# Dilated attention on TensorE: the two heads of a pair take turns block by block, on opposite halves of the array

## The chip, the cores and the metric

The kernel runs on one core of one Trainium2 chip. The metric is the device time of one execution in microseconds (us), as the median of several runs. TensorE is PE in the rows (its weight loads are PEld), VectorE is DVE, ScalarE is ACT, GpSimd is POOL, and SyncE, which issues the weight transfers, is SP.

## The reference, cut to what matters

The model is two blocks of several layers over 512 tokens of width 1024. The change touches one stage of the second block: attention with a causal dilated window. There are twelve heads of width 64 in three groups of four, with (window, dilation) of (128, 1), (512, 4) and (2048, 16).

```python
qb = to_sub(q).reshape(bb, nb, ATTN_BLOCK, h, dh)          # ATTN_BLOCK = 128
kb = band(to_sub(k)); vb = band(to_sub(v))                  # own block and the one before
scores = jnp.einsum('bnqhd,bnkhd->bnhqk', qb, kb) * (dh ** -0.5)
scores = jnp.where(mask[None, :, None], scores, -jnp.inf)
m = jnp.max(scores, axis=-1, keepdims=True)
p = jnp.exp(scores - m)
denom = jnp.sum(p, axis=-1, keepdims=True)
o = jnp.einsum('bnhqk,bnkhd->bnqhd', (p / denom).astype(v.dtype), vb)
lse = (m + jnp.log(denom))[..., 0]
```

The output of a head is its read-out `o` and the logarithm `lse` of its denominator; later the three groups are weighed by a softmax over their `lse`.

## The kernel before

Everything is transposed: channels lie on the 128 partitions, tokens along the free axis. Two heads of width 64 share a tile of 128 partitions, head r = 0 on partitions 0 to 63 and head r = 1 on 64 to 127. Such a tile is called a pair (index u, two of them in each group), and a group (index g) has a stage of its own. The tokens are handled as four blocks of 128 (NB = 4). In group 0 a block of queries sees two blocks of keys (WB = 256), in groups 1 and 2, where the tokens are sorted by residue, only one (WB = 128).

A stage (`dilated_attention`) runs two programs on each engine, woven by a list of turns: the attention of the group (`Dilated`) and a projection that the next stages need (`Flow`). The flow is the bulk of TensorE's work: for each of six output tiles, eight turns of three products of 512 columns (L459, fp32r; the weights are split in an upper part on ACT, L337, and a lower part on DVE, L378). The list spreads the twenty turns of `Dilated` over those of the flow. Within an engine the order is fixed; between engines semaphores decide. A block barrier ends each stage.

For each pair, the attention does this:

- ACT copies the queries, keys and values to tiles of their own (L3202), TensorE turns the values over (L3288), ACT takes them (L3207).
- TensorE makes the scores of head 0 into `ps_s[0]`, and one turn of the list later those of head 1 into `ps_s[1]` (L3298). The queries of a block are the stationary operand, 64 rows by 128 columns, so a head uses only one half of the array's rows. `scored` counts the heads.
- DVE scales and masks a head's scores (L3242), takes the maximum (L3245) and subtracts it (L3247); ACT takes the exponential (L3212). DVE sums (L3254), inverts (L3256) and norms (L3258), head 0 before head 1.
- TensorE turns the probabilities over (L3308), once `normed` says that DVE is done with them; in the first pair of a stage it first runs 12, 9 or 4 products that nobody reads (L57, `keep_busy`). ACT takes them as `pt` (L3220) and spreads the logarithms of the denominators to `lrow` (L3222).
- TensorE makes the read-outs of head r (L3320 for the block before, L3323 for the own block) and its denominators (L3329). Here the stationary operand is 128 rows by 64 columns, and head r writes partitions 64r to 64r + 63 of `ps_o` and of `ps_l` (the latter is `ps_v` in the rows). Head 0 has one turn of the list, head 1 the next.
- DVE and ACT take read-outs and denominators (L3271, L3228), which ends the pair (`turn_done`).

Each 128-column product of type f32 stands in the trace as two loads and two matmuls; a transpose stands there once.

Of the kernel before, what the change touches and what calls it, by code (L numbers as in the profile page):

```python
# [10 lines left out]
P = 128  # L11
# [203 lines left out]
class Flow:  # L215
# [152 lines left out]
    def dve(self, dve):  # L368
# [39 lines left out]
        yield from self.turns(dve, first, events)  # L408

    def pe(self, pe):  # L410
        K, nc = self.K, self.K.nc

# [61 lines left out]
def product(K, name, w, n, kt, rhs_hi, rhs_lo, t0, T, on_act, on_dve, nxt, extra="", side=None, rms_of=None,  # L474
            busy=0):

    nc = K.nc
    with ExitStack() as c:
        f = Flow(K, c, name, w, n, kt, rhs_hi, rhs_lo, t0, T, on_act, on_dve, nxt, extra, side, rms_of)
        unread = c.enter_context(nc.psum_tensor(f"{name}_unread", [P, 512], F32))[:, 0:P] if busy else None  # L480
        with K.block() as block:
            @block.sync
            def _(sp):
                weave([], f.sp(sp))

            @block.gpsimd
            def _(pool):
                if side is not None:
                    side[0].pool(pool)

            @block.scalar
            def _(act):
                weave([], f.act(act))

            @block.vector
            def _(dve):
                weave([], f.dve(dve))

            @block.tensor
            def _(pe):  # L500
                weave([], f.pe(pe))
                if busy:
                    K.keep_busy(unread, busy)
# [2632 lines left out]
class Dilated:  # L3136
# [139 lines left out]
    def pe(self, pe):  # L3276
        nc, K, g, NB, WB = self.nc, self.K, self.g, self.NB, self.WB
        ident = K.ident[:, :]

        def block_of(t, b):  # L3280
            return t[:, b * P:(b + 1) * P]
        for u in range(2):
            if u > 0:
                pe.wait_ge(self.turn_done, u)
            yield
            pe.wait_ge(self.v_in, u + 1)
            for b in range(NB):
                last = nc.tensor.transpose(block_of(self.ps_v, b), block_of(self.vs, b), ident)  # L3288
            last.then_inc(self.v_turned, 1)
            yield  # L3290
            pe.wait_ge(self.qk_in, u + 1)
            for r in range(2):
                half = slice(64 * r, 64 * r + 64)
                for b in range(NB):
                    first = b if g else max(b - 1, 0)
                    spans = [(b * WB, b * P)] if g else [(b * WB, first * P), (b * WB + P, b * P)]
                    for col, key in spans:
                        last = nc.tensor.matmul(self.ps_s[r][:, col:col + P], self.qs[half, b * P:(b + 1) * P],  # L3298
                                                self.ks[half, key:key + P], start=True, stop=True)
                last.then_inc(self.scored, 1)  # L3300
                yield
            yield
            for r in range(2):
                if u == 0 and r == 0:
                    K.keep_busy(self.ps_o[:, 0:P], (12, 9, 4)[g])
                pe.wait_ge(self.normed, 2 * u + r + 1)
                for b in range(self.WS // P):
                    last = nc.tensor.transpose(block_of(self.ps_s[r], b), self.p[:, r, b * P:(b + 1) * P], ident)  # L3308
                last.then_inc(self.p_turned, 1)
                yield  # L3310
            pe.wait_ge(self.vt_in, u + 1)
            for r in range(2):
                n = 2 * u + r
                half = slice(64 * r, 64 * r + 64)
                pe.wait_ge(self.pt_in, n + 1)
                for b in range(NB):
                    both = g == 0 and b > 0
                    if both:
                        at = (b - 1) * P + 64 * r
                        nc.tensor.matmul(self.ps_o[half, b * P:(b + 1) * P], self.vt[:, at:at + 64],  # L3320
                                         self.pt[:, r, b * WB:b * WB + P], start=True, stop=False)
                    at = b * P + 64 * r
                    last = nc.tensor.matmul(self.ps_o[half, b * P:(b + 1) * P], self.vt[:, at:at + 64],  # L3323
                                            self.pt[:, r, (b + 1) * WB - P:(b + 1) * WB], start=not both, stop=True)
                if r:
                    last.then_inc(self.o_done, 1)
                pe.wait_ge(self.rows, n + 1)
                for b in range(NB):
                    last = nc.tensor.matmul(self.ps_l[half, b * P:(b + 1) * P], self.lrow[:, r, b, :], ident,  # L3329
                                            start=True, stop=True)  # L3330
                if r:
                    last.then_inc(self.l_done, 1)
                yield
            yield


# [506 lines left out]
```

## Time and profile before

| | |
|---|---|
| Median of 3 runs | 2849.68 us (2845.45 to 2850.74) |
| The profiled execution | 2852.88 us |
| Its span in the trace | 2851.1 us |
| PE busy | 2660.7 us, 93% of the span |
| DVE, ACT busy | 1666.8 us (58%), 1007.7 us (35%) |
| Granted TensorE clock, mean | 0.979 of full speed |
| The three dilated stages | 2480 to 2659 us of the span |

Read the table so: TensorE is the engine that is nearly always busy, and the three stages of the change are 179 us, 6% of the span. Whether a change of TensorE's work there moves the end is seen from where TensorE itself waits inside those stages.

### The profile page before, as it was taken

What the parts mean: (1) busy time and instruction counts of PE and PEld (TensorE: products, weight loads), DVE (VectorE), ACT (ScalarE), POOL (GpSimd) and SP (SyncE); (2) the same over time, 40 slices, a digit from 0 to 9 for tenths busy, and PEclk for the clock granted to TensorE, in tenths of its full rate; (3) what the DMA queues carried; (4) which work ended last, traced back from release to release, by engine and by line L of the source; (5) the groups of instructions that cost most, each with busy time, mean ns of one, the idle gap of its engine ahead of it and who ended that gap; (6) DMA issues with size and microseconds to landing.
All of it is one profiled execution on the core that took longest, in us unless ns stands there. A gap on an engine that the chain in (4) does not pass through costs nothing. (4 is left out here: it accounts for less than half of the span.)

```text
span 2851.1 us, 37621 instructions
## 1 busy us (share of the span) xinstructions
PE 2660.7 (93%) x15331; PEld 2237.1 (78%) x15331; DVE 1666.8 (58%) x2729; ACT 1007.7 (35%) x1392; POOL 55.4 (2%) x108
## 2 busy tenths in 40 slices
PE   7999888999999999889999999988889897999997
PEld 3888787888888888756579999866778886877786
DVE  4888774466667766443347657466655563343634
ACT  4226545332212223344343323255422223334532
POOL 0100000000010000000000000000000000000000
PEclk9999999999999999999999999999999998999999
DMA  6640002223343332210034443212200000211232
GB/s 230 194 152 16 23 9 80 91 83 95 116 150 104 101 108 81 86 38 8 1 104 138 156 127 114 96 59 74 77 8 16 16 9 30 96 56 58 73 99 78
DMA packets 61950, 231.62 MB, mean 81 GB/s; under 512 B 6865, under 2 KB 9553, under 8 KB 61138
## 3 DMA queue, kind: packets, MB, share of 16 engines
q1 hardware_dynamic: 46802, 174.68, 18.5%
q0 software_dynamic: 14976, 54.53, 6.0%
q8 instruction: 122, 2.00, 0.3%
q14 instruction: 50, 0.41, 0.0%
HBM read 227.08 MB, written 2.10 MB: 80 GB/s over the span
## 5 line engine op out<-in xcount | busy, mean ns | idle before, releaser
L378 DVE TENSOR_TENSOR w_lo<-w_raw,w_hi 128x1024 fp32r<-128x1024 f32 (+4 forms) x284 | 346.9, 1221 | 395.6 <-ACT w_hi L337 392.6
L337 ACT ACTIVATE w_hi<-w_raw 128x1024 fp32r<-128x1024 f32 (+4 forms) x284 | 297.7, 1048 | 224.2 <-PE late_acc L459 87.2
L459 PE MATMUL mid_acc<-mid_h_hi,w_hi 128*128 128x258 f32 x832 | 279.4, 336 | 1.5 <-DVE mid_od_fq L627 1.0
L459 PE MATMUL mid_acc<-mid_h_hi,w_lo 128*128 128x258 f32 x832 | 279.0, 335 | 0.0
L459 PE MATMUL mid_acc<-mid_h_lo,w_hi 128*128 128x258 f32 x832 | 277.1, 333 | 0.0
L459 PE MATMUL late_acc<-late_h_hi,w_hi 128*128 128x258 f32 x704 | 199.3, 283 | 0.0
L459 PE MATMUL late_acc<-late_h_hi,w_lo 128*128 128x258 f32 x704 | 198.4, 282 | 0.0
L459 PE MATMUL late_acc<-late_h_lo,w_hi 128*128 128x258 f32 x704 | 197.6, 281 | 0.0
L459 PEld LDWEIGHTS mid_acc<-mid_h_hi,w_hi 128*128 128x128 f32 x832 | 157.3, 189 | 19.3 <-issue 2.4
L459 PEld LDWEIGHTS mid_acc<-mid_h_lo,w_hi 128*128 128x128 f32 x832 | 157.5, 189 | 18.6 <-issue 1.2
L459 PEld LDWEIGHTS mid_acc<-mid_h_hi,w_lo 128*128 128x128 f32 x832 | 156.8, 188 | 16.1
L459 PEld LDWEIGHTS late_acc<-late_h_lo,w_hi 128*128 128x128 f32 x704 | 133.6, 190 | 0.5 <-issue 0.5
L459 PEld LDWEIGHTS late_acc<-late_h_hi,w_hi 128*128 128x128 f32 x704 | 133.1, 189 | 0.5 <-issue 0.5
L459 PEld LDWEIGHTS late_acc<-late_h_hi,w_lo 128*128 128x128 f32 x704 | 132.7, 188 | 0.0
L459 PE MATMUL mid_acc<-mid_y_hi,w_hi 128*128 128x256 f32 (+1 forms) x384 | 128.8, 335 | 3.5 <-DVE w_lo L378 1.9
L459 PE MATMUL mid_acc<-mid_y_lo,w_hi 128*128 128x256 f32 (+1 forms) x384 | 128.9, 336 | 0.0
L459 PE MATMUL mid_acc<-mid_y_hi,w_lo 128*128 128x256 f32 (+1 forms) x384 | 128.7, 335 | 0.0
L131 DVE CUSTOM_DVE_ANT_0 mid_scratch<-mid_side_raw,mid_rows 128x1024 f32<-128x1024 f32 x96 | 117.4, 1223 | 1.7
L459 PE MATMUL dq_acc<-s_h_hi,w_hi 128*128 128x512 f32 x200 | 87.7, 438 | 20.8 <-DVE w_lo L378 16.6
L2906 ACT ACTIVATE dr_low<-dr_bank 128x512 f32<-128x512 f32 x48 | 28.7, 598 | 169.7 <-PE dr_bank L3036 169.7
L459 PE MATMUL qvz_acc<-ev_h_hi,w_hi 128*128 128x256 f32 (+1 forms) x256 | 87.2, 341 | 1.5 <-DVE ev_h_lo L921 1.5
L459 PE MATMUL qvz_acc<-ev_h_lo,w_hi 128*128 128x256 f32 (+1 forms) x256 | 86.9, 339 | 0.0
(563 smaller groups left out, 6309.4 us busy)
## 6 DMA issues: line engine op xcount, KB each, us to landing
w_raw<-in_up SPq DMA_DIRECT2D x88, 512.0 KB, 3.5
mid_side_raw<-in_ada_t POOLq DMA_DIRECT2D x48, 512.0 KB, 3.8
w_raw<-in_down SPq DMA_DIRECT2D x32, 704.0 KB, 4.0
qvz_side_raw<-in_ada_t POOLq DMA_DIRECT2D x32, 512.0 KB, 3.8
w_raw<-in_dn_qkv SPq DMA_DIRECT2D x25, 512.0 KB, 3.2
late_side_raw<-in_ada_t POOLq DMA_DIRECT2D x24, 512.0 KB, 3.8
w_raw<-in_da SPq DMA_DIRECT2D x18, 512.0 KB, 3.3
w_raw<-in_ev_qvz SPq DMA_DIRECT2D x16, 512.0 KB, 3.5
```

Of the source, the lines that this page charges most:

```text
L131: nc.vector.tensor_tensor_reduce(out=self.scratch, in0=self.raw[:, j, :], in1=self.rows[:, m, :], scale=1.0, scalar=0.0, op0=ALU.mult, op1 ...
L337: nc.scalar.activation(K.whi[:, g % 2, 0:width], K.raw[:, g % 2, 0:width], ACT.Copy).then_inc(K.hi_done, 1)
L378: nc.vector.tensor_tensor(K.wlo[:, g % 2, 0:width], K.raw[:, g % 2, 0:width], K.whi[:, g % 2, 0:width].bitcast(F32), ALU.subtract).then_in ...
L459: last = nc.tensor.matmul(self.acc[i % len(self.acc)][:, at:at + width], left[:, j, cols], right[k][:, moving:moving + width], start=(k == ...
L2906: nc.scalar.activation(XL[G][:, :], bank[G][0][:, :], ACT.Copy).then_inc(A[G].empty, 1)
```

## The change

The loops over blocks and heads change places. The scores of both heads of a pair are now one burst, in which the heads alternate for each block of keys; the burst stands in the turn of head 0, and `scored` is raised by 2 at its end. The read-outs and the denominators of both heads are likewise one burst, in the turn of head 1. No product is added or taken away, and nothing changes on the other engines.

```diff
-            for r in range(2):
-                half = slice(64 * r, 64 * r + 64)
-                for b in range(NB):
-                    first = b if g else max(b - 1, 0)
-                    spans = [(b * WB, b * P)] if g else [(b * WB, first * P), (b * WB + P, b * P)]
-                    for col, key in spans:
+
+            for b in range(NB):
+                first = b if g else max(b - 1, 0)
+                spans = [(b * WB, b * P)] if g else [(b * WB, first * P), (b * WB + P, b * P)]
+                for col, key in spans:
+                    for r in range(2):
+                        half = slice(64 * r, 64 * r + 64)
                         last = nc.tensor.matmul(self.ps_s[r][:, col:col + P], self.qs[half, b * P:(b + 1) * P],
                                                 self.ks[half, key:key + P], start=True, stop=True)
-                last.then_inc(self.scored, 1)
-                yield
+            last.then_inc(self.scored, 2)
+            yield
+            yield
             yield
...
-            for r in range(2):
-                n = 2 * u + r
-                half = slice(64 * r, 64 * r + 64)
-                pe.wait_ge(self.pt_in, n + 1)
-                for b in range(NB):
-                    both = g == 0 and b > 0
-                    if both:
+            pe.wait_ge(self.pt_in, 2 * u + 1)
+            yield
+
+            pe.wait_ge(self.pt_in, 2 * u + 2)
+            for b in range(NB):
+                both = g == 0 and b > 0
+                if both:
+                    for r in range(2):
                         at = (b - 1) * P + 64 * r
...
-                pe.wait_ge(self.rows, n + 1)
-                for b in range(NB):
-                    last = nc.tensor.matmul(self.ps_l[half, b * P:(b + 1) * P], self.lrow[:, r, b, :], ident,
-                                            start=True, stop=True)
-                if r:
-                    last.then_inc(self.l_done, 1)
-                yield
+            last.then_inc(self.o_done, 1)
+            pe.wait_ge(self.rows, 2 * u + 2)
+            for b in range(NB):
+                for r in range(2):
+                    last = nc.tensor.matmul(self.ps_l[64 * r:64 * r + 64, b * P:(b + 1) * P], self.lrow[:, r, b, :],
+                                            ident, start=True, stop=True)
+            last.then_inc(self.l_done, 1)
+            yield
```

The first pair of group 0 on TensorE, before: the scores of the two heads (`da_ps_s`, eight products a head) with three turns of the flow between them.

```order
L459 MATMUL da_acc<-s_h_hi,w_lo 128x512
L3298 MATMUL da_ps_s<-da_ks,da_qs 128x128 x8
L459 MATMUL da_acc<-s_h_hi,w_hi 128x512
L459 MATMUL da_acc<-s_h_lo,w_hi 128x512
L459 MATMUL da_acc<-s_h_hi,w_lo 128x512
...
L3298 MATMUL da_ps_s<-da_ks,da_qs 128x128 x8
```

And in the changed kernel, where the same line is L3299:

```order
L459 MATMUL da_acc<-s_h_hi,w_hi 128x512
L459 MATMUL da_acc<-s_h_lo,w_hi 128x512
L459 MATMUL da_acc<-s_h_hi,w_lo 128x512
L3299 MATMUL da_ps_s<-da_ks,da_qs 128x128 x16
L459 MATMUL da_acc<-s_h_hi,w_hi 128x512
```

The sixteen products stand where the first eight stood; the second place is gone, so head 0's scores are complete eight products later in TensorE's order, and head 1's nine products of the flow earlier.

The read-outs and denominators of the same pair on TensorE, before: this group of rows stands there twice, once for each head, with three turns of the flow between.

```order
L3323 MATMUL da_ps_o<-da_pt,da_vt 64x128
L3320 MATMUL da_ps_o<-da_pt,da_vt 64x128
L3323 MATMUL da_ps_o<-da_pt,da_vt 64x128
L3320 MATMUL da_ps_o<-da_pt,da_vt 64x128
...
L3329 MATMUL da_ps_v<-ident,da_lrow 64x128 x4
```

In the changed kernel (L3323 is now the block before, L3327 the own block, L3333 the denominators):

```order
L3327 MATMUL da_ps_o<-da_pt,da_vt 64x128 x2
L3323 MATMUL da_ps_o<-da_pt,da_vt 64x128 x2
L3327 MATMUL da_ps_o<-da_pt,da_vt 64x128 x2
L3323 MATMUL da_ps_o<-da_pt,da_vt 64x128 x2
...
L3333 MATMUL da_ps_v<-ident,da_lrow 64x128 x8
```

Each x2 is head 0 and head 1 in turn. The whole burst stands at the place of head 1's, with nine more products of the flow ahead of it than head 0's had.

## Rows read from the trace of the kernel before

**Rows 1.** The page: span and busy time of each engine.

```profile
span 2851.1 us, 37621 instructions
...
PE 2660.7 (93%) x15331; PEld 2237.1 (78%) x15331; DVE 1666.8 (58%) x2729; ACT 1007.7 (35%) x1392; POOL 55.4 (2%) x108
```

**Rows 2.** Sum over the three stages: length, busy time of each engine.

```profile
sum 179.00, PE 165.01 PEld 133.28 DVE 80.69 ACT 74.16 POOL 0.00; mean PE 55.00 PEld 44.43 DVE 26.90 ACT 24.72 POOL 0.00
```

**Rows 3.** Groups by shape, 2480 to 2659: count, busy us, mean ns, idle before.

```profile
L3298 PE MATMUL da_ps_s<-da_ks,da_qs 64*128 64x128 f32 x128 | 17.4, 281 | 0.0
L3298 PEld LDWEIGHTS da_ps_s<-da_ks,da_qs 64*128 64x128 f32 x128 | 15.1, 187 | 4.3 <-issue 4.3
L3323 PE MATMUL da_ps_o<-da_pt,da_vt 128*64 128x128 f32 x96 | 15.0, 279 | 0.0
L3329 PE MATMUL da_ps_v<-ident,da_lrow 128*64 128x128 f32 x96 | 12.4, 273 | 0.0
...
L3323 PEld LDWEIGHTS da_ps_o<-da_pt,da_vt 128*64 128x64 f32 x96 | 10.5, 136 | 4.3 <-issue 4.3
...
L3320 PE MATMUL da_ps_o<-da_pt,da_vt 128*64 128x128 f32 x24 | 4.6, 272 | 0.0
```

**Rows 4.** Timeline of PE, group 0, first pair: start, us from first to last.

```profile
2485.34 0.40 PE L459 MATMUL da_acc<-s_h_hi,w_lo 128*128 128x512 f32 x1
2485.66 2.05 PE L3298 MATMUL da_ps_s<-da_ks,da_qs 64*128 64x128 f32 x16
2487.64 0.50 PE L459 MATMUL da_acc<-s_h_hi,w_hi 128*128 128x512 f32 x1
2487.98 0.39 PE L459 MATMUL da_acc<-s_h_lo,w_hi 128*128 128x512 f32 x1
2488.21 0.40 PE L459 MATMUL da_acc<-s_h_hi,w_lo 128*128 128x512 f32 x1
...
2499.54 1.10 PE L3308 MATMUL da_ps_s<-ident,da_p 128*128 128x128 f32 x8 [1.27 <-DVE da_p L3258]
```

**Rows 5.** Timeline of PEld, the read-outs of the same pair.

```profile
2504.91 0.19 PEld L3323 LDWEIGHTS da_ps_o<-da_pt,da_vt 128*64 128x64 f32 x2 [0.36 <-issue]
...
2506.39 0.90 PEld L3329 LDWEIGHTS da_ps_v<-ident,da_lrow 128*64 128x64 f32 x8
```

**Rows 6.** Timeline of DVE, the same pair: each head's scores, and when they come.

```profile
2487.83 1.23 DVE L3242 SCALAR_TENSOR_TENSOR da_p<-da_ps_s,da_msk 128x1024 f32<-128x1024 f32 x1 [4.62 <-PE da_ps_s L3298]
...
2492.01 1.23 DVE L3242 SCALAR_TENSOR_TENSOR da_p<-da_ps_s,da_msk 128x1024 f32<-128x1024 f32 x1 [0.45 <-PE da_ps_s L3298]
```

**Rows 7.** Timelines of DVE and PE, group 0, second pair.

```profile
2526.66 1.22 DVE L3242 SCALAR_TENSOR_TENSOR da_p<-da_ps_s,da_msk 128x1024 f32<-128x1024 f32 x1
...
2533.05 1.97 PE L3308 MATMUL da_ps_s<-ident,da_p 128*128 128x128 f32 x8 [3.35 <-DVE da_p L3258]
```

**Rows 8.** PE in two stretches there: length, busy us, granted clock, DMA.

```profile
2529.70:2533.05 3.35, 0.01 (x1) 0.94 0.00 0
2533.05:2536.00 2.95, 2.95 (x11) 0.50 0.00 0
```

**Rows 9.** Timelines of DVE and PE, group 1, first pair.

```profile
2559.06 0.69 DVE L3242 SCALAR_TENSOR_TENSOR da_p<-da_ps_s,da_msk 128x512 f32<-128x512 f32 x1 [1.14 <-PE da_ps_s L3298]
...
2563.17 0.69 DVE L3258 TENSOR_TENSOR da_p<-da_p,da_inv 128x512 f32<-128x512 f32 x1
...
2564.49 0.60 PE L3308 MATMUL da_ps_s<-ident,da_p 128*128 128x128 f32 x4
```

**Rows 10.** Timelines of DVE and PE: group 1, second pair, and group 2, first pair.

```profile
2591.65 0.69 DVE L3258 TENSOR_TENSOR da_p<-da_p,da_inv 128x512 f32<-128x512 f32 x1
...
2592.40 0.66 PE L3308 MATMUL da_ps_s<-ident,da_p 128*128 128x128 f32 x4
...
2619.53 0.66 PE L3308 MATMUL da_ps_s<-ident,da_p 128*128 128x128 f32 x4 [0.38 <-DVE da_p L3258]
```

More of the change, by code:

```diff
@@ L3311, in pe @@
             pe.wait_ge(self.vt_in, u + 1)
-            for r in range(2):
-                n = 2 * u + r
-                half = slice(64 * r, 64 * r + 64)
-                pe.wait_ge(self.pt_in, n + 1)
-                for b in range(NB):
-                    both = g == 0 and b > 0
-                    if both:
+            pe.wait_ge(self.pt_in, 2 * u + 1)
[5 more added lines that the diff above has]
+                    for r in range(2):
                         at = (b - 1) * P + 64 * r
-                        nc.tensor.matmul(self.ps_o[half, b * P:(b + 1) * P], self.vt[:, at:at + 64],
+                        nc.tensor.matmul(self.ps_o[64 * r:64 * r + 64, b * P:(b + 1) * P], self.vt[:, at:at + 64],
                                          self.pt[:, r, b * WB:b * WB + P], start=True, stop=False)
+                for r in range(2):
                     at = b * P + 64 * r
-                    last = nc.tensor.matmul(self.ps_o[half, b * P:(b + 1) * P], self.vt[:, at:at + 64],
+                    last = nc.tensor.matmul(self.ps_o[64 * r:64 * r + 64, b * P:(b + 1) * P], self.vt[:, at:at + 64],
                                             self.pt[:, r, (b + 1) * WB - P:(b + 1) * WB], start=not both, stop=True)
-                if r:
-                    last.then_inc(self.o_done, 1)
-                pe.wait_ge(self.rows, n + 1)
-                for b in range(NB):
-                    last = nc.tensor.matmul(self.ps_l[half, b * P:(b + 1) * P], self.lrow[:, r, b, :], ident,
-                                            start=True, stop=True)
-                if r:
-                    last.then_inc(self.l_done, 1)
-                yield
+            last.then_inc(self.o_done, 1)
+            pe.wait_ge(self.rows, 2 * u + 2)
+            for b in range(NB):
+                for r in range(2):
+                    last = nc.tensor.matmul(self.ps_l[64 * r:64 * r + 64, b * P:(b + 1) * P], self.lrow[:, r, b, :],
+                                            ident, start=True, stop=True)
+            last.then_inc(self.l_done, 1)
+            yield
             yield
```

## The prediction

> **What bounds the kernel now.** I read the page first: TensorE is busy for 93% of the span, DVE for 58%, ACT for 35% [rows 1], so the end moves with TensorE's own order of work. In the sum over the three dilated stages it is busy for 165.0 of 179.0 us [rows 2]. The groups by shape then give what the change handles: 128 records of scores, and 96 + 24 + 96 = 216 records of read-outs and denominators; a product of 128 columns is two records [rows 3]. Last come the timelines. The reader is to see two things there: how fast such records follow each other, and where TensorE waits for DVE. It does so at the first transposes of a pair (L3308): 1.27 us in the first pair of group 0 [rows 4], 3.35 in its second [rows 7], 0.38 in the first pair of group 2 [rows 10]. Those waits say where time won on TensorE is worth nothing, and where scores that come late cost their full delay.
>
> **The pace of the records.** The burst of sixteen score records lasts 2.05 us [rows 4]. Its last matmul begins about 0.27 before its end and its first stream about 0.10 after its start, so a record takes (2.05 - 0.37) / 15 = 0.112. The loads of the denominators, eight in 0.90 us with a mean of 0.137 [rows 3, 5], follow each other every (0.90 - 0.137) / 7 = 0.109 us. Where no stream is in the way, at the start of the read-outs, the second of two loads of 64 columns begins 0.19 - 0.137 = about 0.054 after the first [rows 5]. So a load of 64 columns holds the loading path for 0.054, the stream of 128 columns is what makes 0.109. A load of 128 columns (187 ns against 136 [rows 3]) is 0.051 longer, about 0.105: in the scores load and stream are about equally long and lie under each other.
>
> **The change, part by part.** Between bursts and the flow there is a toll. Into the scores, the step from the last product of the flow is 2485.66 - 2485.34 = 0.32 instead of 0.23; out of them, the last record begins at 2485.66 + 0.10 + 15 x 0.112 = 2487.44, the flow at 2487.64 and its second product 0.34 later, so 0.09 + 0.11 too much [rows 4]. Together 0.30. The change removes one of two bursts of scores and one of two of read-outs in each of six pairs.
>
> No row shows alternating halves, so their pace is bounded from both sides: 0.109 to 0.112 (nothing overlaps; what rows 4 and 5 show) down to half of it (two halves stream at once), and above it what a load costs that no stream covers, 0.054 or 0.105 more. I take for the forecast that the halves stream together but that there is one loading path, since that is the only limit besides the stream that the rows show. Then a read-out or denominator record costs its load, 0.055, and a score record still about 0.110.
>
> *Read-outs and denominators.* 216 x (0.109 - 0.055) = 11.7 us, and six tolls of 0.30 = 1.8. Nothing hides TensorE's time there: after them it goes on with the flow, and the next waits (for the values' copies, a chain on ACT that starts from a flow tile of TensorE and moves with it) shift along. The probabilities and the logarithms' rows that the burst needs are made by ACT while the nine more products of the flow run. Gain 13.5.
>
> *Scores.* Here something is late. DVE's first head begins when the burst of its scores ends, and now that burst is both heads': 16 records more in group 0 (16 x 0.112 = 1.8 us), 8 in groups 1 and 2 (0.9). Queued behind this wait on DVE are the scaling, maximum and subtraction of both heads, the flow's L378, and the sum, inverse and norm of head 0, for which TensorE's L3308 waits.
> - Group 0, first pair: head 0's three steps end at 2492.01 - 0.45 = 2491.56 and DVE then waited 0.45 for head 1 [rows 6]. Now 1.8 later and without that wait: +1.4 us at L3308, all of it on TensorE, which waits there already.
> - Group 0, second pair: DVE goes through without a wait [rows 7], so the whole 1.8.
> - Group 1, first pair: DVE waited 1.14 for head 1 [rows 9], more than 0.9. DVE is done at 2563.86, TensorE comes at 2564.49 [rows 9]: not bound by DVE, it keeps its toll, -0.3. Group 2, first pair, waits 0.38 for the same chain [rows 10]: 1.14 - 0.9 = 0.2 earlier, -0.2.
> - Second pairs of groups 1 and 2 (one pattern): norm done at 2592.34, L3308 at 2592.40 [rows 10], DVE-bound: +0.9 each.
>
> Sum: 1.4 + 1.8 - 0.3 - 0.2 + 0.9 + 0.9 = +4.5 us. The toll saved there is lost in the waits.
>
> *The clock.* In the 2.95 us after the wait of 3.35, during which TensorE had done nothing, the granted clock is 0.50, that is 1.2 instead of 2.4 GHz [rows 8]; half of 2.95 us, about 1.4, is lost. In the first pair the 12 unread products (L57) stand ahead of the wait, and 1.27 leaves the clock alone. With the change this wait becomes 1.27 + 1.4 + 0.3 = 3.0, close to the one that did fall. I count one more fall, +1.4. The wait of the second pair grows to about 5.5; its fall is there already.
>
> Sum: -13.5 + 4.5 + 1.4 = **-7.6 us**. The profiled execution took 2852.9, which gives 2845.3; it lies 3.2 over the median of the runs, 2849.7, so against the median I forecast 2842.
>
> **Two rules of the skill.** The rows show loads of 64 columns every 0.109 us at a duration of 0.137, under the stream of the product before, on the same rows of the array [rows 3, 5]. The Trainium skill (TensorE: Matmul & The Clock Gate, Part 3, what overlaps and what doesn't) says that a load overlaps with matmuls in flight only when it targets other rows. The read-outs of both heads use all rows, so by that rule none of their loads would be covered, and the sum would be a loss; the trace disagrees for loads to the same half. Another page, TensorEngine Tiling (Array Packing), Key Properties, says that different tiles load and multiply in parallel. By that the scores would be halved too, which is the first rival below; no run here shows it yet.
>
> **The rivals.**
> - *Everything halves, loads too.* For it: head halves of the scores share neither rows nor output banks. Then both heads' scores are there when head 0's were before (32 x 0.056 = 16 x 0.112). L3308 comes 0.45 earlier in the first pair of group 0, 1.2 in that of group 1 (16 x 0.056 and a toll), 1.1 in that of group 2 (its wait for head 1 gone), and not at all in the second pairs, where DVE binds: -2.8, with -13.5 and +1.4 for the clock -14.9, or **2835**.
> - *Partial overlap in the read-outs.* A head's two records share a half, so if the queue is strictly in order, the load for the other half starts only when the second stream does. Then records alternate between 0.109 and 0.055, mean 0.082: 216 x 0.027 + 1.8 = 7.6 gained, +4.5 and +1.4 against it: -1.7, or **2848**. For it: every load in the rows starts with a stream, never ahead of one.
> - *No overlap at all.* The change then does not do what it says: only the tolls are won, -1.8 + 4.5 + 1.4 = +4.1, or **2854**.
> - *Slower: the load is exposed whenever the half changes.* That is at 108 of the 216 records and 64 of the 128. The read-outs cost 108 x 0.054 = 5.8, less 1.8. The scores' burst is 16 x 0.105 = 1.7 (or 0.8) longer still: first and second pair of group 0 +3.1 and +3.5, of group 1 +0.6 and +1.75, of group 2 +0.65 and +1.75. Sum +15.4, with the clock +16.8: **2866**. From no overlap at +4.1 it needs little, about 13% of a load exposed at each change, to be slower than a measurement's noise.
> - *Only the scores' halves overlap* (rows may be split, columns not): -2.8 - 1.8 + 1.4 = -3.2, **2846**.
>
> **How the numbers follow.** A measurement of this kernel can tell about 0.2%, 5.7 us. Chances: everything halves 0.28, the forecast 0.27, partial 0.17, none 0.13, only scores 0.05, exposed loads 0.10. Faster than 2844: the first and most of the second, 0.50. Within 0.2%: the rest of the second, partial, scores only and nearly all of none, 0.37. Slower: 0.13. The range takes in all but the exposed loads: from 2835 without the fall of the clock and some scatter, 2832, to 2854 with the same, 2855. The forecast's own range is 2839 to 2845, by the clock and by a pace of 0.050 to 0.065.
>
> **What the changed profile would show.** The burst of 44 read-out and denominator records in group 0 lasts 2.5 us if the pace is 0.055 (4.9 without overlap, 3.7 partial). The 32 score records last 3.6 as forecast, 1.9 if both halves load at once. The wait at L3308 in group 0 is 3.0 and 5.5 us in either case, and a stretch at clock 0.50 follows the first. DVE no longer waits between the heads (L3242, 0.45 and 1.14). I am wrong if scores halve, if read-outs keep 0.109, or if the waits at L3308 are shorter than before.

## The result, and the profile after

The changed kernel is faster: 2829.37 us as the median of 5 runs (2821.82 to 2832.98) against 2849.68 us (5 runs, 2843.14 to 2851.27), a ratio of 0.9932 with a 95% interval of 0.9916 to 0.9949. Forecast were 2842 us in a range of 2832 to 2855.

The page of the profiled execution (2832.98 us), and the sum over the three stages with length and busy times, which answer to [rows 1] and [rows 2]:

```profile
span 2831.2 us, 37621 instructions
...
PE 2636.0 (93%) x15331; PEld 2220.0 (78%) x15331; DVE 1666.4 (59%) x2729; ACT 1007.4 (36%) x1392; POOL 55.4 (2%) x108
```

```profile
sum 163.00, PE 143.75 PEld 116.87 DVE 80.26 ACT 73.16 POOL 0.00; mean PE 47.92 PEld 38.96 DVE 26.75 ACT 24.39 POOL 0.00
```

TensorE is busy for 21 us less in the stages (165.0 before), but they are only 14.5 us shorter: counted from the first product of the flow to the first one behind the third stage, 2658.61 - 2480.91 = 177.70 us before and 2640.37 - 2477.12 = 163.25 us now. The groups by shape (count, busy us, mean ns) answer to [rows 3]:

```profile
L3299 PE MATMUL da_ps_s<-da_ks,da_qs 64*128 64x128 f32 x128 | 8.8, 281 | 0.0
L3299 PEld LDWEIGHTS da_ps_s<-da_ks,da_qs 64*128 64x128 f32 x128 | 7.6, 187 | 2.2 <-issue 2.2
L3327 PE MATMUL da_ps_o<-da_pt,da_vt 128*64 128x128 f32 x96 | 7.6, 279 | 0.0
L3333 PE MATMUL da_ps_v<-ident,da_lrow 128*64 128x128 f32 x96 | 6.3, 273 | 0.0
```

Every group keeps its count and its mean duration, and its busy time is halved (17.4, 15.1, 15.0 and 12.4 before): the records lie over each other in pairs, the loads of the scores too. The timelines of PE, PEld and DVE in group 0, first pair, answer to [rows 4, 6]:

```profile
2481.88 2.06 PE L3299 MATMUL da_ps_s<-da_ks,da_qs 64*128 64x128 f32 x32
2483.86 0.50 PE L459 MATMUL da_acc<-s_h_hi,w_hi 128*128 128x512 f32 x1
...
2495.24 1.64 PE L3310 MATMUL da_ps_s<-ident,da_p 128*128 128x128 f32 x8 [2.96 <-DVE da_p L3258]
```

```profile
2481.88 1.86 PEld L3299 LDWEIGHTS da_ps_s<-da_ks,da_qs 64*128 64x128 f32 x32 [0.36 <-issue]
```

```profile
2484.06 1.22 DVE L3242 SCALAR_TENSOR_TENSOR da_p<-da_ps_s,da_msk 128x1024 f32<-128x1024 f32 x1 [4.64 <-PE da_ps_s L3299]
...
2487.71 1.22 DVE L3242 SCALAR_TENSOR_TENSOR da_p<-da_ps_s,da_msk 128x1024 f32<-128x1024 f32 x1
```

Thirty-two score records take the 2.06 us that sixteen took, and 32 loads the 1.86 us of sixteen. So DVE gets head 0's scores as early as before (6.9 us after the stage's first product in both kernels) and has head 1's at once; its wait of 0.45 us is gone. TensorE, which now comes 2.2 us earlier, waits 2.96 us for DVE instead of 1.27. In the second pair it waits 5.56 instead of 3.35. In all, TensorE's waits for DVE in the three stages grow from 5.0 to 11.6 us; that is why 21 us less work makes them only 14.5 us shorter.

The loads at the start of the read-outs answer to [rows 5]:

```profile
2504.26 0.20 PEld L3327 LDWEIGHTS da_ps_o<-da_pt,da_vt 128*64 128x64 f32 x4 [0.35 <-issue]
```

Four loads now take the time of two (0.19 us before, x2). The whole burst of 44 records of read-outs and denominators takes 2.55 us, from 2504.26 to the flow's next product at 2506.81, as one head's 22 records did before. The stretches of PE behind the two waits, as length, busy us, granted clock, DMA:

```profile
2495.24:2499.00 3.76, 3.76 (x14) 0.55 0.04 15
...
2527.61:2533.00 5.39, 5.39 (x17) 0.50 0.00 0
```

The clock is at 1.2 GHz behind both; before it was so behind the second alone, and for 2.95 us [rows 8].

Of the 19.9 us between the two spans, 14.5 are the stages'. The other 5.4 lie where both kernels run the same instructions. In the twelve profiled executions of this study the span outside the stages is 2663 to 2677 us whatever the kernel (2673.4 in the one of before, 2668.0 here), so this remainder is within the scatter. It goes with the clock: by the granted clock in the two traces TensorE was at 1.2 GHz for 117 us outside the stages before and for 107 now. Half of the difference, 5.0 us as an estimate, is nearly all of the 5.4. The longest of the twelve (2677 us) had 135 us at the low clock there, the shortest (2663 us) 104.

### The profile page after: what moved, and what is told of

Same layout as the page of the kernel before. It is cut to its first block and busy times, and to the rows that moved or that the text cites. A ratio compares the mean times of both kernels' runs of the same rounds, so it can differ in the third digit from the quotient of the medians.

```text
span 2831.2 us, 37621 instructions
## 1 busy us (share of the span) xinstructions
PE 2636.0 (93%) x15331; PEld 2220.0 (78%) x15331; DVE 1666.4 (59%) x2729; ACT 1007.4 (36%) x1392; POOL 55.4 (2%) x108
```

## Experiments

The runs of a table were timed beside the kernel before. "Stages" is the length as counted above, from one profiled execution of each.

| kernel | stages, us | ratio to before, 95% interval |
|---|---|---|
| before | 177.7 | 1 |
| changed | 163.3 | 0.9932 (0.9916 to 0.9949) |
| changed, again | 163.1 | 0.9955 (0.9937 to 0.9972) |
| scores only | 177.4 | 1.0008 (0.9994 to 1.0022) |
| read-outs and denominators only | 163.8 | 0.9946 (0.9929 to 0.9963) |
| bursts by head | 170.3 | 0.9976 (0.9961 to 0.9992) |
| turns of two blocks | 167.4 | 0.9964 (0.9948 to 0.9980) |
| changed, waits filled | 159.0 | 0.9934 (0.9916 to 0.9952) |
| changed, scores first | 153.5 | 0.9914 (0.9898 to 0.9929) |
| scores first and filled | 151.9 | 0.9921 (0.9904 to 0.9938) |
| before, head 0's scores first | 173.6 | 0.9973 (0.9958 to 0.9987) |
| head 0's first, read-outs alternating | 159.7 | 0.9918 (0.9891 to 0.9945) |

**The changed kernel again** (no edit).

> The changed kernel once more, beside the other runs. If the 14.5 us by which its three stages are shorter are all that the change does, ten runs of it together come out nearer -15 than -20 us, and the rest of the span differs by the places and number of the stretches at the low clock, in either direction. If something outside the stages is faster for a reason, the same parts of the span are shorter again, by the same amounts.

Measured: 2832.21 us (6 runs) against 2846.48, -14.3 us by the medians and about -13 by the ratio, and 163.1 us of stages. By their ratios the first comparison gave about -19 us and this one -13, together (11 runs) about -16, nearer to -15 than to -20. Their intervals overlap between -14.5 and -18 us; the stages give -14.5. Nothing outside them was faster again by a fixed amount: the part ahead of them ended at 2477.1 us in the first execution and at 2475.4 in this one, and between 2471.7 and 2485.1 in those of the other kernels.

**Scores only.** The second half of the change is undone, as in this diff against the changed kernel:

```diff
-            pe.wait_ge(self.pt_in, 2 * u + 1)
-            yield
...
+            for r in range(2):
+                n = 2 * u + r
+                half = slice(64 * r, 64 * r + 64)
+                pe.wait_ge(self.pt_in, n + 1)
```

> Only the scores of the two heads alternate; read-outs and denominators stand as before. Theory H (halves stream and load at once): the burst of 32 score records of group 0 lasts about 2.0 us, and six such bursts save 128 x 0.056 = 7.2 us of TensorE's time and 1.8 of tolls, but most of it turns into longer waits at the first transposes (3.0 and 5.5 us in group 0), so the three stages become only 2.8 us shorter, of which longer stretches at the low clock take back up to 2.8: 0 to -3 us against before. Rival G (TensorE's time counts wherever it is saved): -9 us. Rival L (one loading path, as I forecast): the burst lasts 3.6 us and the kernel is 4 to 6 us slower.

Measured: 2848.86 against 2846.48 us, no difference, and stages 0.3 us shorter. The waits of PE, in total, number and longest, of this kernel:

```profile
PE da_ps_s L3310 <- DVE da_p L3258: 11.6, 5, 5.6
```

Before, the same wait was 3 times, 5.0 us in total. The score burst did shrink (32 records in group 0 hold TensorE for 1.99 us). Of the 9 us that the expectation puts on bursts and tolls, 6.6 went straight into the wait for DVE. The stretches of low clock took most of the rest: from the first transposes (L3310) to the second TensorE needs 4.62 and 5.61 us in the two pairs of group 0, against 3.02 and 4.41 before, 2.8 us more. Time saved ahead of a wait that another engine sets is not time.

**Read-outs and denominators only.** The first half is undone; the scores have their two places again.

```diff
-            for b in range(NB):
-                first = b if g else max(b - 1, 0)
...
+            for r in range(2):
+                half = slice(64 * r, 64 * r + 64)
+                for b in range(NB):
...
-            last.then_inc(self.scored, 2)
-            yield
-            yield
+                last.then_inc(self.scored, 1)
+                yield
```

> Only read-outs and denominators alternate; the scores stand as before. Theory H: the burst of 44 records of group 0 lasts 2.5 us, the waits at the first transposes stay 1.3 and 3.4 us, the clock falls only where it did, and the stages are 216 x 0.054 + 1.8 = 13.5 us shorter: 2836 us. Rival: if what the result shows beyond the stages (some 5 us) belongs to the change, it must appear here or in the other half of it.

Measured: 2830.31 us, ratio 0.9946, and stages 13.9 us shorter, with the waits of before (PE for DVE 5.0 us, three times). This half of the change is nearly all of its gain: 13.9 of the 14.5, and 0.3 + 13.9 = 14.2 with the scores. The 5 us beyond the stages appear in neither half: this one is about 15 us faster by its ratio, the scores only are no faster.

**Bursts by head.** Both bursts stand where the change puts them, but the loop over heads is outside again:

```diff
             pe.wait_ge(self.pt_in, 2 * u + 2)
-            for b in range(NB):
-                both = g == 0 and b > 0
-                if both:
-                    for r in range(2):
+            for r in range(2):
+                half = slice(64 * r, 64 * r + 64)
+                for b in range(NB):
+                    both = g == 0 and b > 0
...
```

> Both bursts stand where the change puts them, with one increment each, but inside a burst all of head 0 comes before all of head 1, so that the half changes once. Theory H (the gain is the alternation): records keep their 0.112 and 0.109, twelve tolls or 3.6 us are won, the late scores cost 4.5 + 1.8, the clock up to 2.8: the kernel is 3 to 6 us slower than before. Rival M (the gain is the merging of the bursts): 10 us or more faster.

I expected 3 to 6 us slower and it is 0.24% faster, with stages 7.4 us shorter. The timeline of PE in group 1, read-outs (L3326) and denominators (L3333), shows the main reason:

```profile
2564.72 1.25 PE L3326 MATMUL da_ps_o<-da_pt,da_vt 128*64 128x128 f32 x13
2565.71 0.32 PE L3333 MATMUL da_ps_v<-ident,da_lrow 128*64 128x128 f32 x1
2565.82 0.27 PE L3326 MATMUL da_ps_o<-da_pt,da_vt 128*64 128x128 f32 x1
2565.87 0.27 PE L3333 MATMUL da_ps_v<-ident,da_lrow 128*64 128x128 f32 x1
2565.93 0.27 PE L3326 MATMUL da_ps_o<-da_pt,da_vt 128*64 128x128 f32 x1
2565.98 0.27 PE L3333 MATMUL da_ps_v<-ident,da_lrow 128*64 128x128 f32 x1
2566.03 0.27 PE L3326 MATMUL da_ps_o<-da_pt,da_vt 128*64 128x128 f32 x1
2566.09 1.20 PE L3333 MATMUL da_ps_v<-ident,da_lrow 128*64 128x128 f32 x13
2567.22 0.50 PE L459 MATMUL da_acc<-s_h_hi,w_hi 128*128 128x512 f32 x1
```

The read-outs at 2565.82, .93 and 2566.03 are head 1's last three, and each has a denominator record of head 0 beside it, which in program order comes after all of them. TensorE takes records for the free half ahead of records that wait for their own half, some three deep. A change of half is therefore worth 0.35 to 0.4 us; there are three of them in this burst, which takes 2.50 us (32 x 0.109 + 0.2 = 3.7 without overlap, 1.90 in the changed kernel), and one in each burst of scores (3.43 us in group 0 against 3.8).

There is a second reason. I had put the low clock at up to 2.8 us, and it cost nothing more than before. Here are the wait at the first transposes of group 0 and the stretch behind it, as length, busy us, granted clock, DMA:

```profile
2492.68:2495.64 2.96, 0.01 (x1) 1.00 0.48 162
2495.64:2499.00 3.36, 3.36 (x21) 1.00 0.03 13
```

The wait is as long as in the changed kernel, 2.96 us, and no fall of the clock follows it, where there it was at 1.2 GHz. A wait of this length can bring the fall and need not.

**Turns of two blocks.** How near must the other half's work be?

```diff
-            for b in range(NB):
+            for b0 in range(0, NB, 2):
+                for r in range(2):
+                    half = slice(64 * r, 64 * r + 64)
+                    for b in (b0, b0 + 1):
...
```

> The changed kernel with turns of two blocks instead of one (head 0's two, then head 1's two) in scores, read-outs and denominators. The bursts by head showed an overlap of about three records at each change of half. Theory W (a record for the other half goes ahead of at most about three that wait for their own half): in group 1 the 32 records of read-outs and denominators take 1.9 us, as when each block alternates, since a turn is only four records long, and the stages take 163 to 164 us. Rival N (only the next record is taken ahead, three was another effect): 2.7 us or more, and the stages 168 us or more.

PE in group 0, scores, and in group 1, read-outs and denominators:

```profile
2481.72 2.82 PE L3300 MATMUL da_ps_s<-da_ks,da_qs 64*128 64x128 f32 x32
2484.46 0.50 PE L459 MATMUL da_acc<-s_h_hi,w_hi 128*128 128x512 f32 x1
```

```profile
2566.17 1.15 PE L3329 MATMUL da_ps_o<-da_pt,da_vt 128*64 128x128 f32 x16
2567.09 1.09 PE L3337 MATMUL da_ps_v<-ident,da_lrow 128*64 128x128 f32 x16
2568.12 0.50 PE L459 MATMUL da_acc<-s_h_hi,w_hi 128*128 128x512 f32 x1
```

Where a turn is four records (group 1) the burst takes 1.95 us, as good as 1.90. In group 0 a turn of two blocks is eight score records, which I had not counted in the expectation of the stages: 2.74 us, between 1.98 and 3.43, and stages of 167.4 instead of 163 to 164. By the stages alone this is nearer to rival N (168 or more); but about 1 us of them is low clock (5.60 and 5.50 us between the transposes of the two pairs, against 4.61 and 5.60 in the changed kernel). The lengths of the bursts decide. Three changes of half at 0.35 us make 2.7 of the 3.8 us, as measured. A reach of one record would leave about 3.5, and 2.7 or more in group 1.

**The waits filled.** The number of unread products ahead of the first transposes is raised:

```diff
-                if u == 0 and r == 0:
-                    K.keep_busy(self.ps_o[:, 0:P], (12, 9, 4)[g])
+                if r == 0:
+                    K.keep_busy(self.ps_o[:, 0:P], ((24, 9, 6), (24, 5, 5))[u][g])
```

> The changed kernel with more products that nobody reads ahead of the first transposes (24 in both pairs of group 0 instead of 12 and none; 9, 6, 5 and 5 in the others), so that they fill the waits of 2.96, 5.56 and 1.29 us. Theory H: the waits themselves stay DVE's, but the granted clock stays at 2.4 GHz through group 0, and the records after the waits, which took 1.6 and 2.6 us too long in the changed kernel, keep their pace: 4 us less in the stages (163.2 to 159), 18 to 19 us under before. Rival: the clock's stretches cost only their own scatter, or the fill delays what follows: no gain over the changed kernel, 163 us or more.

PE in the two stretches of group 0 around the filled waits, as length, busy us, granted clock, DMA:

```profile
2490.00:2497.00 7.00, 6.72 (x53) 1.00 0.24 77
2521.00:2530.00 9.00, 8.80 (x65) 1.00 0.06 23
```

The clock stays up and the stages are 159.0 us, 4.2 less than in the changed kernel. That is what low clock cost it. The fill itself delays nothing: the first transposes begin 18.1 us into group 0 in both kernels, and those of the second pair 1.6 us earlier than in the changed kernel, which is the cost of its first fall. The whole kernel does not show the 4 us: 2830.28 us, ratio 0.9934, between the 0.9932 and 0.9955 of the changed kernel.

With the low clock's cost taken out of each kernel's stages (1.4 us before, 4.2 in the changed kernel and with scores only, 1.5 with read-outs only) the change is worth 17.2 us, the scores 3.2 of them and the read-outs and denominators 14.0.

**Scores first.** The burst of scores changes places with the values' transposes:

```diff
             yield
-            pe.wait_ge(self.v_in, u + 1)
-            for b in range(NB):
-                last = nc.tensor.transpose(block_of(self.ps_v, b), block_of(self.vs, b), ident)
-            last.then_inc(self.v_turned, 1)
-            yield
             pe.wait_ge(self.qk_in, u + 1)
...
             last.then_inc(self.scored, 2)
             yield
+            pe.wait_ge(self.v_in, u + 1)
+            for b in range(NB):
+                last = nc.tensor.transpose(block_of(self.ps_v, b), block_of(self.vs, b), ident)
+            last.then_inc(self.v_turned, 1)
+            yield
```

> The changed kernel with the scores' burst one turn earlier than the values' transposes. Theory D (after the change DVE's chain between scores and first transposes binds TensorE, so time is won by starting that chain earlier): the chain starts 1.6 us earlier in every pair, the waits in group 0 become about 1.2 and 4.2 us, one stretch at the low clock goes, and the stages lose 7 us more than with the change (163.2 to about 156). Rival: the wait moves to ACT's copies of queries and keys or to the values' take-over, and the stages stay within 1 us of 163.

Measured: 2824.85 against 2849.15 us, ratio 0.9914, stages 153.5 us. The waits of PE:

```profile
PE da_ps_s L3310 <- DVE da_p L3258: 8.2, 4, 4.1
...
PE da_ps_s L3294 <- ACT da_ks L3202: 0.6, 2, 0.5
```

The stages are 9.7 us shorter than with the change, where I expected 7. The wait for DVE falls from 11.6 to 8.2 us (1.11 and 4.14 in group 0, as expected). The 3.7 us of waiting for ACT's copies of the values are gone, and 0.6 for the keys' has come; ACT copies queries and keys before the values, and I had not counted this. The first fall of the clock is gone too (3.01 us between the transposes of the first pair, 4.62 in the second), 2.6 us less. These three make 9.1 of the 9.7.

**Scores first and filled.**

```diff
-                if u == 0 and r == 0:
-                    K.keep_busy(self.ps_o[:, 0:P], (12, 9, 4)[g])
+                if r == 0:
+                    K.keep_busy(self.ps_o[:, 0:P], ((17, 9, 4), (18, 6, 6))[u][g])
```

> The scores first, as in the run before, and unread products that fill the waits left over (17 and 18 in group 0, 6 in the second pairs of the other groups). If both theories hold the stages take about 154 us, and the kernel is some 23 us under before: the best of all. If the fill is longer than a wait, that stage is longer than with scores first alone.

Measured: stages 151.9 us, the shortest of all and 1.6 under scores first alone, what its one stretch of low clock cost (4.62 us instead of 3.01), but 2826.02 us for the kernel, which the runs do not tell from scores first alone.

**Head 0's scores first, nothing alternating**, and **the same with alternating read-outs.** In the kernel before, the values' transposes move behind the first scores:

```diff
-            pe.wait_ge(self.v_in, u + 1)
-            for b in range(NB):
-                last = nc.tensor.transpose(block_of(self.ps_v, b), block_of(self.vs, b), ident)
-            last.then_inc(self.v_turned, 1)
-            yield
...
                 last.then_inc(self.scored, 1)
                 yield
+                if r == 0:
+                    pe.wait_ge(self.v_in, u + 1)
+                    for b in range(NB):
+                        last = nc.tensor.transpose(block_of(self.ps_v, b), block_of(self.vs, b), ident)
+                    last.then_inc(self.v_turned, 1)
+                    yield
```

> The kernel before, nothing alternating, with the scores of head 0 one turn earlier than the values' transposes (those of head 1 stay where they were). If starting DVE's chain early were worth the same with or without the change, the stages would be 10 us shorter, as they were from the changed kernel to scores first. Theory D (before the change the chain binds only in part, since head 1's scores hold it): 3 to 5 us shorter, 173 to 175 us, the wait in group 0's second pair about 2.5 us and the wait for ACT's copies ahead of a pair mostly gone.

> The same order with read-outs and denominators alternating as in the change; the scores stay by head. Beside the run with scores first, in which the scores alternate too (153.5 us), it tells what alternating scores are worth once DVE's chain starts early. Theory D: the 13.9 us of the read-outs add to the 4 of the order, 159 to 160 us, so alternating scores are worth about 6 us there, against 0.3 when they alone were changed. Rival: they are worth nothing anywhere, 154 us.

Measured: stages of 173.6 us, 4.1 shorter than before, and of 159.7 us with the read-outs alternating; in both the wait in group 0's second pair is 2.81 us and 0.5 us of waiting for ACT's copies is left. The 13.9 us of the read-outs add to the order's. From here to scores first, where the scores alternate too, in one burst, are 6.2 us of stages: alternating scores, worth 0.3 us in the change (3.2 but for the low clock), are worth six where the chain starts early. The low clock costs the same 1.6 us in both of these kernels. The whole kernels (2824.11 against 2846.92, and 2824.85 against 2849.15 in the other comparison) are too wide to show these 6 us.

## Why the prediction was wrong

The way was right and the size was not. The step that failed is the choice between the bounds of the pace: "I take for the forecast that the halves stream together but that there is one loading path", from which followed "a score record still about 0.110". The runs showed that the loads of the two halves run at once too.

- *The pace of the scores.* Measured 0.056 us (32 records in 1.98 us), not 0.110. The rows of before showed loads and streams of equal length under each other, from which one can read how long a load is, but not that two loads for different halves exclude each other. I took the lack of a row for a limit. With 0.056 the +4.5 us for late scores become about -3: the stages with scores only are 0.3 us shorter, with longer stretches of low clock that cost some 2.8.
- *The read-outs.* -13.5 forecast, -13.9 measured alone. The pace of 0.055 was the right number, but by luck. I had it as loads that follow each other at 0.054 on one path. The trace has four loads of 0.137 in 0.20 us, so all begun within 0.063, where one path would need 3 x 0.054 = 0.16; after that the two heads' loads come in pairs every 0.109. A load of 64 columns happened to be half as long as a stream of 128, so both pictures gave one pace. Only the scores, whose loads are as long as their streams, tell them apart.
- *The waits.* 3.0 and 5.5 us forecast, 2.96 and 5.56 measured. This does not speak for the forecast's pace, since the prediction has these waits "in either case". In the first pair it had DVE 1.4 us late and TensorE 0.3 early; measured, DVE is 0.5 us early and TensorE 2.2. DVE's 0.45 and 1.14 us between the heads are gone, as forecast.
- *The clock.* One more fall came, where it was expected, though the bursts by head, with the same wait, had none; and the one that was there already grew too. From the first transposes to the second, TensorE needed 3.02 us at full clock before (2499.54 to 2502.56) and 4.41 in the second pair, and needs 4.61 and 5.60 us in the two pairs now. That is 1.6 + 2.6 = 4.2 us of low clock against the 1.4 of before: 2.8 more, not 1.4. The filled kernel shows the same 4.2.
- *The first rival*, everything halves at 2835 us, had the right mechanism and the sum -2.8 - 13.5 + 1.4 = -14.9 where the stages show -14.5. Its chance of 0.28 was the highest, yet I called 2842 the forecast, with 0.27. The lower end of the range, 2832, already stood for this rival, and the measured 2829.37 lies 2.6 us under it; that last part is not the mechanism. The first comparison came out 5.6 us under 2835, and the second at -13 to -14 us; the difference lies outside the stages, in the scatter.
- *The partial rival* assumed that a record waits for all those ahead of it. Bursts by head and turns of two blocks show that it does not. Exposed loads (0.10) and no overlap (0.13) are ruled out by the halved busy times.
- *The two pages.* The rule of the Trainium skill that different tiles load and multiply in parallel (TensorEngine Tiling (Array Packing), Key Properties) agrees with the trace: 32 loads in 1.86 us. The rule of the Trainium skill that a load overlaps matmuls in flight only when it targets other rows (TensorE: Matmul & The Clock Gate, Part 3, what overlaps and what doesn't) does not agree with it: the loads of the read-outs, all on 128 rows, are covered as well, every pair of records at 0.109 us.

## What to carry to other kernels

Where two products use different halves of the array, by rows or by columns, let them alternate closely: with f32 products of 128 columns the pair costs what one did. It did so with two and with four records of one half together; with eight together part of the gain was lost (2.74 us against 1.98). Ask then who waits for the result. Here 14 of 14.5 us came from the products with the flow behind them, and the scores' saving turned into waits for DVE and low clock until their burst was moved ahead. Where an idle stretch grows by such a change, look at the granted clock behind it; unread products were worth 4 us in the stages.

## What the runs showed that I had not expected

TensorE reorders across halves. At a change of half in program order, about three records of the next half run beside the last three of the one before, worth 0.35 to 0.4 us each time. Even the kernel with bursts by head, in which nothing alternates, is 7.4 us shorter in its stages for that reason and for the tolls, though its scores come later (its first transposes begin 0.9 us later than before). What sets the reach at about three is open.

The clock does not fall after every wait of one length. At the first transposes of group 0 waits of 2.94 to 2.96 us were followed by 1.2 GHz in both profiled executions of the changed kernel, with scores only and with turns of two blocks, and not with bursts by head. Whether the fall comes there again in another execution was not measured.
